# Issuing 96 loads of conditioning weights from GpSimd's software queue instead of SyncE's, in a hybrid decoder layer

## The reference

```python
c_act = jax.nn.silu(c)
mod = c_act @ w_ada[l] + b_ada[l]
sh1, sc1, g1, sh2, sc2, g2 = [m[:, None, :] for m in jnp.split(mod, N_MOD, axis=-1)]
h = rms_norm(x, norm1_w[l]) * (1.0 + sc1) + sh1
proj = h @ w_in[l]                       # 2048 x 7168
y_attn = dilated_window_attention(qa, ka, va)   # 8 heads, rotary on the first 32 of 128 channels
y_rec = hgrn2(hq, hf, hi, hg, lb_all[l], gnorm_w[l])   # 8 heads, gated recurrence
x = x + g1 * (jnp.concatenate([y_attn, y_rec], axis=-1) @ w_out[l])
h = rms_norm(x, norm2_w[l]) * (1.0 + sc2) + sh2
u = causal_depthwise_conv(h @ w_up[l], conv_w[l], conv_b[l])
x = x + g2 * ((jax.nn.silu(gate) * up) @ w_down[l])
return rms_norm(x, final_norm_w)
```

## Time and profile before

| | us |
|---|---|
| median of 3 timed runs | 1360.34 |
| lowest and highest of them | 1351.99 and 1361.84 |
| the profiled execution's own time | 1352.04 |
| its span, first to last instruction | 1350.2 |
| mean granted clock of TensorE in it | 0.971 |
| pieces in use on VectorE (L1373), start of first and last | 170.1 and 577.3 |

### The profile page before, as it was taken

The page is one execution under the profiler, slowest core; times in us unless marked ns, Lnnn a source line. Parts: engine busy times, 40 slices in busy tenths (PEclk is TensorE's granted clock), DMA queues, the critical chain, the costliest instruction groups (busy, mean ns, idle before and its releaser), DMA issues.

```text
span 1350.2 us, 20741 instructions
## 1 busy us (share of the span) xinstructions
PE 1276.2 (95%) x7269; PEld 1123.7 (83%) x7269; DVE 1008.5 (75%) x1295; ACT 604.4 (45%) x794; POOL 51.9 (4%) x99
## 2 busy tenths in 40 slices
PE   3888899999998999989999999999999999999996
PEld 3877799998997787868888888888888878888885
DVE  3777698899976689868978888897868766545453
ACT  3223355444546554455544444444444534444342
POOL 2000000022021000000000000000000000000000
PEclk9688899999999999999999999999999999999999
DMA  8999588888777779957777777777666675555552
GB/s 321 378 342 339 182 295 265 266 276 272 256 261 246 239 257 374 340 175 248 255 244 233 235 243 231 239 233 237 191 192 187 187 264 192 197 190 196 194 192 104
DMA packets 151699, 329.77 MB, mean 244 GB/s; under 512 B 11221, under 2 KB 11974, under 8 KB 150738
## 3 DMA queue, kind: packets, MB, share of 16 engines
q1 hardware_dynamic: 147392, 315.92, 71.0%
q0 software_dynamic: 3360, 9.98, 2.1%
q10 hardware_dynamic: 882, 3.00, 0.6%
HBM read 323.09 MB, written 4.19 MB: 242 GB/s over the span
## 4 chain that ended last, share of the span: by engine, by line
PE 85%; DVE 6%; ACT 3%; issue 3%; DMA 2%; ACTq 0%; DVEq 0%
PE bank L1189 24%; PE bank L1191 12%; PE bank L1212 6%; PE bank L1210 6%; PE bank L1211 6%; PE bank L956 5%; PE bank L958 4%; PE bank L957 4%; PE bank L946 4%; PE bank L945 4%; PE bank L943 4%; DVE acc_c L1309 3%; DMA x<-in_x 1%; PE bank L914 1%; PE bank L990 1%
## 5 line engine op out<-in xcount | busy, mean ns | idle before, releaser
L617 ACT ACTIVATE whi<-wraw 128x1024 fp32r<-128x1024 f32 x408 | 432.5, 1060 | 635.9 <-PE bank L1191 238.3
L1297 DVE TENSOR_TENSOR wlo<-wraw,whi 128x1024 fp32r<-128x1024 f32 x404 | 493.8, 1223 | 277.9 <-ACT whi L617 275.6
L1189 PE MATMUL bank<-h,whi 128*128 128x512 f32 x1408 | 490.1, 392 | 2.7 <-issue 2.7
L1191 PE MATMUL bank<-h,wlo 128*128 128x256 f32 x1408 | 395.1, 281 | 0.0
L1189 PEld LDWEIGHTS bank<-h,whi 128*128 128x128 f32 x1408 | 264.3, 188 | 60.8 <-issue 2.8
L1191 PEld LDWEIGHTS bank<-h,wlo 128*128 128x128 f32 x1408 | 267.1, 190 | 0.0
L943 PE MATMUL bank<-h,whi 128*128 128x256 f32 x512 | 148.2, 289 | 3.2 <-DVE h L1328 3.2
L945 PE MATMUL bank<-h,whi 128*128 128x256 f32 x512 | 145.4, 284 | 0.0
L946 PE MATMUL bank<-h,wlo 128*128 128x256 f32 x512 | 145.4, 284 | 0.0
L1210 PE MATMUL bank<-whi,act_hi 128*128 128x512 f32 x352 | 137.0, 389 | 0.3 <-DVE evt L1584 0.3
L1212 PE MATMUL bank<-whi,act_lo 128*128 128x512 f32 x352 | 137.0, 389 | 0.0
(11 more groups left out here) (224 smaller groups left out, 1307.1 us busy)
## 6 DMA issues: line engine op xcount, KB each, us to landing
wraw<-in_w_up SPq DMA_DIRECT2D x176, 512.0 KB, 3.8
araw<-in_w_ada SPq DMA_DIRECT2D x128, 512.0 KB, 5.2
wraw<-in_w_in SPq DMA_DIRECT2D x112, 512.0 KB, 4.5
wraw<-in_w_down SPq DMA_DIRECT2D x88, 512.0 KB, 4.2
pc<-in_w_ada SPq DMA_DIRECT2D x64, 512.0 KB, 9.6
wraw<-in_w_out SPq DMA_DIRECT2D x32, 512.0 KB, 6.0
x<-in_x ACTq DMA_DIRECT2D x1, 2048.0 KB, 16.0
x<-in_x POOLq DMA_DIRECT2D x1, 2048.0 KB, 11.9
```

What stands on the lines that cost most here:

```text
L617: act.activation(whi[:, slot], wraw[:, slot], ACT.Copy).then_inc(s_hi, 1)
L1189: pe.matmul(out, whi[:, slot, k, cols], h[:, kk].rearrange("p a t -> p (a t)"), start=(kk == 0), stop=False, skip_group_check=True)
L1191: last = pe.matmul(out[:, 0:SEQ], wlo[:, slot, k, cols], h[:, kk, 0, :], start=False, stop=(kk == KT - 1), skip_group_check=True)
L1297: dve.tensor_tensor(wlo[:, slot], wraw[:, slot], whi[:, slot].bitcast(F32), ALU.subtract).then_inc(s_lo, 1)
```

## The change

`load_piece` moves from SyncE's stream to GpSimd's. In GpSimd's loop the loads of pieces with PIECE_AT[p] up to s are issued at the head of step s, before the gather, scatter or wait of that step. The wait for piece p-4 stays, and so does VectorE's place for each piece. The 32 pieces for g2 stay on SyncE's queue and get semaphores `s_ag` of their own, so that no semaphore is raised by two queues.

```diff
+        s_ag = [sem(f"s_ag{j}") for j in range(RING)]
...
-            p = 0
             for v in range(PER_CHUNK * (CHUNKS - 1) + RING, UP0):
-                while p < len(PIECE_AT) and PIECE_AT[p] + 5 <= v:
-                    load_piece(p)
-                    p += 1
                 if v < PROJ_UNITS:
                     load_in(v)
...
-                sp.dma_start(araw[:, slot], src).then_inc(s_a[slot], 16)
+                sp.dma_start(araw[:, slot], src).then_inc(s_ag[slot], 16)
...
+            def load_piece(p):
+                mod, half = HALVES[p // 16]
+                row = p % 16 * P
+                if p < RING:
+                    gp.wait_ge(s_h, KT)
+                gp.wait_ge(s_ada, p + 1)
+                gp.dma_start(araw[:, p % RING],
+                             w_ada[row:row + P, mod * D + half * AW:mod * D + (half + 1) * AW]).then_inc(s_a[p % RING], 16)
+
+            p = 0
             for s in range(UP0):
+                while p < len(PIECE_AT) and PIECE_AT[p] <= s:
+                    load_piece(p)
+                    p += 1
...
-                dve.wait_ge(s_a[slot], count)
+                dve.wait_ge(s_ag[slot], count)
...
-                        ada(acc_g2, i * 4 + (ph.ada0 + n - 1 + 4), n, i * 16 + (ph.ada0 // RING + 1) * 16,
+                        ada(acc_g2, i * 4 + (ph.ada0 + n - 1 + 4), n, i * 16 + 16,
```

More of the change, by code:

```diff
@@ L442, in load @@
                 sp.dma_start(wraw[:, v % RING], src.rearrange("(k p) n -> p k n", p=P)).then_inc(s_w[v % RING], 16)
[L444 to L451, removed]
             def load_in(v):
```

## The result

The changed kernel took 1364.33 us (median of 18 runs, 1357.78 to 1377.8), the kernel before 1354.07 (18 runs beside it, 1348.98 to 1361.84). The ratio is 1.0065, 95% interval 1.0041 to 1.0089: 8.8 us slower, which is also how far the means are apart (the medians 10.3), inside the 1% that was taken as no change, and inside the range. The profiled execution of the new kernel took 1366.08 us, span 1364.2, mean granted clock 0.975, against 1352.04, 1350.2 and 0.971.

What follows compares the result with a forecast made beforehand. The prediction took TensorE's own work as the bound, VectorE following closely. Terms 2.95 + 2.2 + 0 + 0.5 = 5.65 us, set on the three-run median of 1360.34, gave 1366.0 us; range 1354 to 1385.

Steps and rivals of the forecast that it cites:

- Place A: First rotary block, steps 57 and 60: pieces late behind gather and scatters, TensorE's second scores lose 2.95 us.
- Place B: Second rotary block, steps 65 to 69: piece behind the scatters 2.61 us late, TensorE's second scores lose 2.2 us.
- The removal: SyncE's stream: taking out 96 issues and their waits is worth nothing, as the queue waited for VectorE anyway.
- GpSimd's 48 us of issues: GpSimd: 96 added issues, some 48 us, are hidden on an engine busy 51.9 of 1350.2 us.
- Rival 1: The software queue is slow for pieces, landing time up to 6.5 us: about 25 us lost, 1385 us; chance 0.22.
- L = 5.2: Time in us from a piece's issue on GpSimd to its landing, taken from SyncE's median; bounds 3.6 and 9.4.
- Place C: Third rotary block: a piece behind the scatters is 1.3 us late, with 1.45 to spare: loss 0.
- Place D: Step 116: the piece behind x's 2 MB load is up to 3.7 us late; loss 0.5 us, bounds 0 and 3.7.
- rival 3: Place D decides: steps 116 to 120 each end up 3.7 us late, TensorE's x1 waits grow, 1369.2 us; chance 0.10.
- The clock: TensorE at half clock for 10.2 us after a gap: up to 5.1 us per place, only in the range.
- signs of being wrong: Median landing over 6 us, issues over 0.6, no idle before L991, longer stop before L1095, half-clock row 310 to 345.
- Rival 2: Not slower: GpSimd's queue has no weights, so pieces land in 3.8 us; 1360.5 us; chance 0.16.

Runs made afterwards that it cites:

- e6: The kernel before, pieces on SyncE's queue, with x's reload cut into four column parts at steps 115, 123, 131 and 139; ratio 1.0019 to the kernel before.
- e1: The changed kernel with GpSimd issuing each piece three steps earlier; 449.7 us from unit 24's end to unit 149's, against 445.8 in the kernel before.
- e2: The changed kernel with pieces issued three steps earlier only below step 96; it loses 3.45 us at unit 123.
- e5: e1 with x's reload cut into four column parts at steps 115, 123, 131 and 139; ratio 1.0017 to the kernel before.
- e8: The kernel before, with GpSimd issuing x's reload only when VectorE has finished the piece of step 114; nothing changed, +0.12 us.
- e12: e1 with the 24 pieces of steps 112 to 136 back on SyncE's queue; 445.55 us from unit 24's end to unit 149's, ratio interval 0.9948 to 1.0035.
- e3: The changed kernel with pieces issued three steps earlier only from step 112 on; 13.84 us lost against the kernel before.
- e4: The changed kernel with every piece issued one step later on GpSimd; +7.15 and +5.75 us at Place A and Place B.
- e7: The changed kernel, without earlier issue, with x's reload cut into four column parts at steps 115, 123, 131 and 139; ratio 1.0064 to the kernel before.
- e9: e1 with x's reload as four DMAs of 512 columns, one behind the other; 448.15 us from unit 24's end to unit 149's.
- e11: e9 with every piece also cut into two DMAs of 512 columns; 448.20 us from unit 24's end to unit 149's.

## Why the prediction was right, and where not

The forecast was 5.65 us on the median, the ratio says 8.8; the sign and places A and B were right, the size low by a third. That the time itself, 1366.0, came within 1.7 us of the 1364.33 measured is luck: the median of three runs that it stood on, 1360.34, was 6.3 over that of 18.

- **The removal is worth 0.** Right: SyncE's wait only moved to the low parts, and e6 shows that even without ScalarE's waits for weights nothing is gained.
- **GpSimd's 48 us of issues are hidden.** Right: 51.3 us more busy, 527 to 560 ns each beside a busy VectorE. Rival 1, the slow software queue, falls by this (its signs were issues over 0.6 us or a median landing over 6) and by e1's median of 4.9. The second half of what the Trainium skill ("SBUF — State Buffer", section "SBUF: two separate sides") says of VectorE and GpSimd agrees with these lengths as it did before.
- **L = 5.2.** The median of all was 5.4, but at the places that count it differs: 4.42 behind the first gather, 6.03 and 6.08 behind the first two scatters (5.09 behind the second gather, 4.92 behind the third scatter). One number for all was the weak step. With the 0.4 us more that the prediction takes from the Trainium skill, its own working gives 0.8 at A and 0.4 at B, 1.2 us and not some 2.
- **Place A** foretold VectorE 1.06 late, then 2.69, then TensorE 2.95 lost. Measured 0.42, 3.48 and 3.07: the first landing shorter, the second longer, and the sum of them nearly right by that.
- **Place B** foretold 2.61 and a loss of 2.2; measured 3.44 and 3.05. This is the term mis-sized through L: at 6.08 its own working gives 3.5 and 3.1.
- **Place C** is 0 as foretold: the piece of step 84 came 0.97 late where 1.3 was foretold (405.75, above), and TensorE lost nothing. In the fourth block VectorE waits 1.27 and 0.20 us, and TensorE doesn't.
- **Place D** is the step that failed. The late piece was foretold within 0 to 3.7 and is 3.02. The reason for taking 0.5, that TensorE has four steps until x1, didn't look at VectorE, which could make up only 0.95 us between this piece and x1 (3.02 late becomes 2.07), nor at the first transposes with 0.15 us to spare. The wait grew by 2.03 less the 0.46 that the second one lost, which is rival 3 in kind. And rival 3 in turn lacked the second cause, the weights that come 2 us later when pieces and x share the other queue.
- **The clock** was left out. The drop behind place B came and cost 1.8 us (4.85 less the gap of 3.05), that behind D 1.4, each 3.4 us long and not 10.2 as in the earlier trace rows, so about a third of the 5.1 that were kept. The others, at units where the gap itself is as before (+1.50, -1.46, +1.31), no term of the sum could have held. Two of the prediction's signs of being wrong did come: the longer stop before L1095, and a half-clock row, at 348.2 just behind the 310 to 345 that it named.
- Rival 2, not slower, needed an L under 4.1; the fastest piece took 3.9, none at the places that count.

## What to carry to other kernels

A DMA moved to another engine's stream inherits whatever that engine waits for: write down for each moved issue what stands ahead of it there and when that is released, and give it one step of lead (here one step took away 8 of the 12.5 us in the trace). Where the DMA engines are full, as here in `w_out`, a second queue is no second road: it changed who was served first, so put urgent and less urgent loads in one queue in the order of their need. And before calling a delay covered, add up the idle time of every engine between it and the next wait that TensorE feels, not only the steps.

## What the runs showed of the hardware that was not expected

**Half-clock stretches come and go behind the same gap.** The gap of 2.31 us before L1029 left the clock at 1.00 in before (window above) and in e1, e2, e5, e6 and e8 to e12; in after, e3, e4 and e7, the four with gaps before L991, 3.4 us at 0.50 followed it and cost 1.5. Between units 24 and 149 such stretches were 3.4, 6.8 or 10.2 us long. The unit 144 loss of about 1.0 comes in exactly the four traces (after, e5, e9, e11) whose last one in `w_out` lasts 10.2 us instead of 6.8. What decides the length, no run here tells.

**Two levels of one code.** From count 149 to 440 of TensorE's semaphore, in `w_up` and `w_down`, the traces take either 619.6 us (before, after, e1, e2, e4, e7, e9 to e12) or 628.7 (e3, e5, e6, e8), with nothing between. One group of TensorE shows it, 700 to 1000 us, before first and then e8 (busy us, mean ns):

```profile
L1189 PE MATMUL bank<-h,whi 128*128 128x512 f32 x867 | 300.6, 391 | 0.0
```

```profile
L1190 PE MATMUL bank<-h,whi 128*128 128x512 f32 x850 | 300.4, 399 | 0.0
```

The granted clock is 1.00 in both windows and TensorE is never idle; each matmul is 2% longer. No trace shows one kernel at both levels, so that it belongs to the execution and not to the kernel is argued, but the times speak for it: the 35 timed runs of before that were made beside e5 to e8 lie from 1348.6 to 1355.1 and from 1358.8 to 1363.7, with none between, and e1, e2 and e3 differ in one number of GpSimd's loop. A difference of 3 us between two kernels is therefore told by the traces' stretch and hardly by 12 timed runs.
